# The last u pair of a Conformer and retention decoder kernel, computed as the first of 21 units of seven half-size products

## What is computed

```python
proj = rms_norm(x) @ w_in                       # 1024 x 6144
a_val, a_gate, q, k, v, g, gate_a, gate_b = split(proj)
u = a_val * sigmoid(a_gate)                     # 512 channels
conv = depthwise_conv31(concat(history, u)) + b_dw
a_out = silu(layer_norm(conv)) @ w_conv_out
o = retention(rotary(q), rotary(k), v)          # chunks of 128, 4 heads
b_out = (silu(g) * rms(o)) @ w_ret_out
h = x + rms_norm((sigmoid(gate_a) * a_out + sigmoid(gate_b) * b_out) @ w_o)
y = h + rms_norm(relu(rms_norm(h) @ w_up)**2 @ w_down)
```

## Time and profile before

| | |
|---|---|
| median of three runs | 1497.71 us (1497.56 to 1498.16) |
| profiled execution: span, first to last instruction | 1495.6 us |
| its mean granted TensorE clock | 0.997 |
| busy TensorE / VectorE / POOL / ACT | 99% / 67% / 56% / 42% |
| third pair begins, first unit begins, second unit begins | 60.95, 106.41, 127.19 us |

### The profile page before, as it was taken

The page is one execution under the profiler, slowest core; times in us unless marked ns, Lnnn a source line. Parts: engine busy times, 40 slices in busy tenths (PEclk is TensorE's granted clock), DMA queues, the critical chain, the costliest instruction groups (busy, mean ns, idle before and its releaser), DMA issues.

```text
span 1495.6 us, 28307 instructions
## 1 busy us (share of the span) xinstructions
PE 1475.2 (99%) x11336; PEld 1455.2 (97%) x11336; DVE 1001.0 (67%) x1251; ACT 635.4 (42%) x929; POOL 842.0 (56%) x571
## 2 busy tenths in 40 slices
PE   8999999999999999999999999999999999999996
PEld 5999999999999999999999999999999999999995
DVE  7999888856545724576715876766657765574847
ACT  5533444344544541131213855556556332332333
POOL 3377776777545653257565445555555655554555
PEclk9999999999999999999999999999999999999998
DMA  6013333322356258621421144566759575454634
GB/s 217 22 42 94 114 114 113 113 80 65 112 176 205 75 200 296 219 80 50 149 78 50 29 149 171 199 237 219 253 193 326 203 285 189 142 208 156 227 107 170
DMA packets 110091, 229.13 MB, mean 153 GB/s; under 512 B 8960, under 2 KB 20992, under 8 KB 108304
## 3 DMA queue, kind: packets, MB, share of 16 engines
q1 hardware_dynamic: 95296, 204.30, 39.7%
q10 hardware_dynamic: 14672, 23.09, 4.6%
HBM read 154.41 MB, written 72.95 MB: 152 GB/s over the span
## 4 chain that ended last, share of the span: by engine, by line
PE 96%; POOL 1%; DMA 1%; ACT 1%; issue 1%; DVE 0%; POOLq 0%; SPq 0%; DVEq 0%; ACTq 0%
PE ps L1476 40%; PE ps L1237 26%; PE ps L1026 16%; PE ps L1402 3%; PE ps L1389 3%; PE ps L1074 2%; PE ps L1164 1%; PE ps L1169 1%; PE ps L1180 1%; PE ps L1166 1%; DMA cva_h<-conv_scratch 1%; PE ps L1147 0%; PE ps L1152 0%; PE ps L1194 0%; POOL w_l L931 0%
## 5 line engine op out<-in xcount | busy, mean ns | idle before, releaser
L1476 PE MATMUL ps<-tx_h,w_h 128*128 128x258 f32 x960 | 271.5, 283 | 0.0
L1476 PE MATMUL ps<-tx_l,w_h 128*128 128x258 f32 x960 | 271.3, 283 | 0.0
L1476 PE MATMUL ps<-tx_h,w_l 128*128 128x258 f32 x960 | 271.1, 282 | 0.0
L996 POOL TENSOR_TENSOR w_l<-raw,w_h 128x512 fp32r<-128x512 f32 x120 | 185.6, 1551 | 147.6 <-ACT w_h L2033 147.1
L1476 PE MATMUL ps<-fx_l,w_h 128*128 128x258 f32 x720 | 203.7, 283 | 0.0
L1476 PE MATMUL ps<-fx_h,w_h 128*128 128x258 f32 x720 | 203.6, 283 | 0.0
L1476 PE MATMUL ps<-fx_h,w_l 128*128 128x258 f32 x720 | 203.4, 282 | 0.0
L1476 PEld LDWEIGHTS ps<-tx_h,w_h 128*128 128x128 f32 x960 | 181.4, 189 | 0.1
L1476 PEld LDWEIGHTS ps<-tx_l,w_h 128*128 128x128 f32 x960 | 181.4, 189 | 0.1
L1476 PEld LDWEIGHTS ps<-tx_h,w_l 128*128 128x128 f32 x960 | 181.2, 189 | 0.0
L2328 DVE SCALAR_TENSOR_TENSOR ps<-u_ext,wdw,ps 128x512 f32<-128x512 f32 x232 | 155.2, 749 | 0.0
(11 more groups left out here) (386 smaller groups left out, 4305.4 us busy)
## 6 DMA issues: line engine op xcount, KB each, us to landing
raw<-wseq_dram SPq DMA_DIRECT2D x260, 256.0 KB, 3.1
quad_scratch<-quad_h SPq DMA_DIRECT2D x16, 774.0 KB, 3.5
tx_h<-quad_scratch SPq DMA_DIRECT2D x12, 1032.0 KB, 10.4
tx_l<-hidden_scratch SPq DMA_DIRECT2D x12, 1032.0 KB, 12.8
gate_scratch<-gst SPq DMA_DIRECT2D x10, 1032.0 KB, 5.0
hidden_scratch<-hq_g SPq DMA_DIRECT2D x8, 1032.0 KB, 7.0
hidden_scratch<-stg_b SPq DMA_DIRECT2D x6, 1032.0 KB, 6.9
hq_g<-hidden_scratch SPq DMA_DIRECT2D x6, 1032.0 KB, 13.1
```

The costliest lines, as they stand in the source:

```text
L996: pool.tensor_tensor(lo, src, hi.bitcast(F32), ALU.subtract).then_inc(q_lo, 1)
L1476: out = pe.matmul(ps[:, 2 * n + s, 0:HC], RINGS[q % RING][wa][:, kk * P:(kk + 1) * P], OPS[x][xb][:, QK * kh + kk, at_:at_ + HC], start=(i ...
```

## The change

Pair 3 is computed as unit 0 of 21 (`X_U = 0`); all other units move one number up. Slots 12 to 15 of the weight stream are now loaded, split and summed as a unit's. The eight half sums of x stand two behind each of the low parts of slots 8, 9 and 10, the seventh behind the first weight sum, the eighth between the third and the fourth low part of unit 0. On ACT the high parts of operands 2 and 3 stand behind slot 10's and slot 11's, 5 ahead of the third weight, 4 within unit 0. VectorE makes 2, 3, 5 and 4 in this order between fewer taps: 17 instead of 29 taps stand before the units, nine in unit 0, ten in unit 1 and eleven in each of units 2 to 9. Gate products are now in units 2 to 5. The product of gate and value of tile 3, and its sample part, stand at the head of unit 1 on VectorE (`u_unit_out`), behind two sigmoids of ACT. The two conv outputs leave one unit later. The first group of the convolution's output product starts with two of its three chunks and takes the third when its bank is free.

```diff
-XU = 20
+XU = 21
-G_AOUT, S_AOUT = 9, 16
+G_AOUT, S_AOUT = 7, 12
+X_U = 0
+U_SLOTS = 12
+OPERAND_AT = {2: 1, 3: 2, 5: 3, 4: 4}
...
@@ POOL
-            for n in range(RAW, 16):
-                if n == 15:
-                    unit_sum(0, 0)
+            for n in range(RAW, U_SLOTS):
                 low_part(n % RAW, n)
                 if n == 2 * RAW:
                     pool.wait_ge(xs_sc, KT)
-                    x_sum(0)
-                if 2 * RAW <= n < 15:
-                    x_sum(n - 2 * RAW + 1)
+                if 2 * RAW <= n < U_SLOTS - 1:
+                    x_sum(2 * (n - 2 * RAW))
+                    x_sum(2 * (n - 2 * RAW) + 1)
+            unit_sum(0, 0)
+            x_sum(6)
...
                 unit_low(v, 2)
+                if v == 0:
+                    x_sum(7)
                 unit_low(v, 3)
@@ TensorE
-            with pe.Fori(0, CT - 2) as i:
-                group8(G_U + 4, S_U + 8, XN, i, i * 4)
-                group8(G_U + 5, S_U + 10, XN, i, i * 4)
+            group8(G_U + 4, S_U + 8, XN)
+            group8(G_U + 5, S_U + 10, XN)
...
-                    taken(pe, G_U + 6 + k)
+                    taken(pe, G_U + 4 + k)
...
                 if v == 0 and 2 <= i <= 5:
-                    pe.wait_ge(xs_lo, i - 1)
+                    pe.wait_ge(xs_lo, OPERAND_AT[i])
...
-                    x_evicted(pe, XU - 1, ("e2", "e7")[c])
-                    x_evicted(pe, XU - 1, "e5")
+                    x_evicted(pe, XU - 1, ("e5", "e2")[c])
@@ ACT
             weight_hi(10)
             x_operand_hi(2)
+            u_gate(2)
             weight_hi(11)
-            u_gate(2)
-            weight_hi(12)
             x_operand_hi(3)
-            weight_hi(13)
-            weight_hi(14)
-            x_operand_hi(4)
-            u_gate(3)
-            weight_hi(15)
...
                 unit_high(v, 4)
+                if v == X_U:
+                    x_operand_hi(4)
...
+                if v == X_U:
+                    x_evicted(act, v, "e2")
+                    act.activation(x_row(v, 0), x_row(v, 0), ACT.Sigmoid).then_inc(u_sg, 1)
...
             unit_high(0, 0)
             unit_high(0, 1)
+            x_operand_hi(5)
             unit_high(0, 2)
-            x_operand_hi(5)
@@ VectorE
             taps(10)
             u_out(1)
             u_sample(1)
-            taps(11)
+            taps(3)
+            x_operand_lo(2)
+            taps(2)
+            x_operand_lo(3)
+            taps(2)
             u_out(2)
             u_sample(2)
-            x_operand_lo(2)
-            taps(8)
-            x_operand_lo(3)
-            u_out(3)
-            x_operand_lo(4)
             x_operand_lo(5)
-            u_sample(3)
...
+                dve.wait_ge(u_sg, 1)
+                for name in ("e5", "e6", "e7"):
+                    x_evicted(dve, X_U, name)
+                for t in range(2):
+                    at_ = HIST + t * HT
+                    dve.tensor_tensor(u_ext[:, CT - 1, at_:at_ + HT], x_row(X_U, 2 + t), x_row(X_U, t), ALU.mult
+                                      ).then_inc(u_x, 1)
+                dve.wait_ge(u_x, 2)
+                u_sample(CT - 1)
...
                 if v < X_KQ[0][0]:
-                    if j == 1:
-                        taps(4 if v < 5 else 5)
-                    if j == 5 and v < 5:
-                        taps(1)
-                    if j == 6:
-                        taps(5 if v < 4 else 6)
+                    if v == X_U:
+                        if j == 1:
+                            x_operand_lo(4)
+                            taps(4)
+                        if j == 6:
+                            taps(5)
+                    else:
+                        if j == 1:
+                            taps(4 if v < 6 else 5)
+                        if j == 5 and v < 6:
+                            taps(1)
+                        if j == 6:
+                            taps(5 if v < 2 else 6)
+                if (v, j) == (X_U + 1, 0):
+                    u_unit_out()
```

More of the change, by code:

```diff
@@ L404, in build @@
         y_st = sem("y_st")
+        u_sg = sem("u_sg")
+        u_x = sem("u_x")
         def done(slot):
@@ L459, in x_loads @@
         def x_loads(v):
-            return 16 * (16 // RAW + v)
+            return 16 * (U_SLOTS // RAW + v)
         XBANKS = [(2, 1, 0)]
@@ L483, in x_rows @@
         def x_rows(v, r, n):
-            if v in X_GATES:
+            if v in X_GATES or v == X_U:
                 k = 4 * (v % 2) + r
-                if v in (13, 14):
-                    k = 4 * (v - 13) + r
+                if v == X_GB[3]:
+                    k = 4 + r
+                if v in X_GB[1:3]:
+                    k = 4 * X_GB[1:3].index(v) + r
                     return gst_c[:, k:k + n, :]
@@ L611, in _ @@
             sp.dma_start(x_in[:, :, 2 * CH:T], xT[:, :, 2 * CH:T]).then_inc(x2_ld, 16)
-            sp.dma_start(hist[:], cacheT).then_inc(hist_ld, 16)
-            for n in range(2 * RAW, 16):
+            sp.dma_start(hist[:], cacheT).then_inc(wdw_ld, 16)
+            for n in range(2 * RAW, U_SLOTS):
                 sp.wait_ge(w_split, n - RAW + 1)
@@ L1294, in _ @@
                 if c == 0:
-                    for n, sub in enumerate((2, 3, 0, 1)):
+                    for n, sub in ((0, 2), (1, 3)):
+                        pe.wait_ge(piece_ld[sub], CV_LD + 16)
+                        for a in range(2):
+                            for b in (1, 2):
+                                pe.matmul(pch(g, b), W[a][:, slot % HL, sub * P:(sub + 1) * P],
+                                          cva_h[:, sub, b * CH:(b + 1) * CH], start=(n == 0 and a == 0), stop=False)
+                    x_evicted(pe, XU - 1, "e7")
+                    for n, sub in ((0, 2), (1, 3)):
+                        for a in range(2):
+                            pe.matmul(pch(g, 0), W[a][:, slot % HL, sub * P:(sub + 1) * P],
+                                      cva_h[:, sub, 0:CH], start=(n == 0 and a == 0), stop=False)
+                    for n, sub in ((2, 0), (3, 1)):
                         pe.wait_ge(piece_ld[sub], CV_LD + 16)
@@ L1299, in _ @@
                                 pe.matmul(pch(g, b), W[a][:, slot % HL, sub * P:(sub + 1) * P],
-                                          cva_h[:, sub, b * CH:(b + 1) * CH], start=(n == 0 and a == 0), stop=False)
+                                          cva_h[:, sub, b * CH:(b + 1) * CH], start=False, stop=False)
                         if n == 2:
-                            x_evicted(pe, XU - 1, "e7")
                             pe.wait_ge(on_n, 6)
@@ L1825, in unit_out @@
                 if v == 0:
-                    taken(act, G_U + 7)
+                    taken(act, G_U + 5)
                 if v == 1:
                     act.wait_ge(xs_lo, 4)
+                if v == 2:
+                    act.wait_ge(u_x, 2)
                 if v in X_KQ[1]:
@@ L2244, in square_half @@
                 if c:
-                    dve.wait_ge(x_sq, 2 * c + half - 1)
+                    dve.wait_ge(x_sq, 2 * c + half + 3)
                 else:
-                    dve.wait_ge(x0_sq, 2 * half + 2)
+                    dve.wait_ge(x_sq, 2 * half + 2)
                 return dve.tensor_tensor(q[:, a:a + 2], q[:, a:a + 2], q[:, a + 2:a + 4], ALU.add)
```

70 lines of the change are left out of this document (34 added, 36 removed).

## The result

The changed kernel takes 1502.46 us (1501.73 to 1502.65), the kernel before in the same runs 1497.73: a ratio of 1.0029, 95% interval 1.0020 to 1.0039. It is slower by 4.7 us, where the forecast was 5.1. The profiled execution spans 1500.6 us, against 1495.6.

The account below looks back on a forecast made before the run. TensorE bounds the kernel, and the change makes it wait for POOL's full queue: 8.1 us of waits less 0.6 and 2.5 gives +5.1, so 1497.7 + 5.1 = 1502.8 us, range 1499.0 to 1505.0.

Parts of the forecast that it names:

- The gain: On TensorE, a 22.73 us pair becomes a 20.21 us unit: 2.52 us saved, at most 3.1 with 0.57 us of waits gone.
- POOL's queue: From 58.87 us to the fourth product's low part: 31.5 us of work, ready at 90.4, wanted at 92.3, slack 1.9 us.
- Who gets the port: VectorE's four all-SBUF low parts each go between two back-to-back POOL instructions, holding POOL 4 x 2.25 = 9.0 us.
- The waits: TensorE waits for POOL's last-slot low part and the first unit's first, fourth and fifth products: 8.1 us in all.
- The bounds: Waits between 5.9 and 8.1 us, so change between +2.8 and +5.1, upper end taken; some other costs taken as nothing.
- the sample at the head of the second unit: Last u tile's sample part may delay the row addition freeing the seventh product's bank: 0.7 us by layout, nothing taken.
- the twelve taps: Taps moved behind, making eleven a unit in units 2 to 5 on VectorE: costed at nothing, though with thin cover.
- (a): Rival: VectorE's low parts fit into POOL's pauses, no wait grows: 1494.6 us, or 1495.2 with some waits; chance 0.05.
- (b): Rival: half of it collides, two of four low parts, 3.6 us of waits less 3.1: 1498.2 us; chance 0.12.
- (d): Rival: VectorE, not POOL, is late, the second product waiting for the u product, adding 1 to 2: 1504; chance 0.08.
- (c): Rival: the clock falls to 1.2 GHz in the 3.0 us stop, +1.0 to +3.9: 1503.8 to 1506.7 us; chance 0.07.

Follow-up runs that it names:

- before_sums_on_dve: The kernel before, with the eight sums of x on VectorE, three low parts in one go and seven taps later: 1496.62 us, ratio 0.9993.
- sums_on_dve: The changed kernel with the eight sums of x on VectorE instead of POOL, low parts regrouped, seven taps later: 1494.71 us, ratio 0.9982 against the kernel before.
- sums_early: The changed kernel with POOL's sums of x begun after four of the eight gains, which come reordered: 1496.72 us, ratio 0.9995 against the kernel before.
- taps_later: The changed kernel with seven VectorE taps moved from between the low parts into units 6 to 9: 1501.14 us.
- lows_together: sums_early with VectorE's second to fourth operands' low parts in one go, seven taps later, the last slot's high part behind two operand parts on ScalarE: 1499.74 us.
- w11_lows_ahead: lows_together with the last slot's high part back ahead on ScalarE and the first unit's first two low parts ahead of its weight sums on POOL: 1499.12 us.
- before_pool_plus: The kernel before plus two unused 512-column POOL instructions behind the sixth sum of x, counted in ScalarE's raised wait: 1500.06 us, ratio 1.0014.
- before_pool_late: The kernel before plus two extra 512-column POOL instructions behind the eighth sum of x, ScalarE's waits unchanged: 1497.42 us, ratio 0.9998.
- pool_plus: The changed kernel plus two more 512-column POOL instructions behind the sixth sum of x, ScalarE's wait raised to count them: 1503.55 us.

## Why the prediction was right

- **The gain.** 22.73 - 20.21 = 2.52 us, capped at 3.1 with the old waits. Shown: the pair of runs with no waits on POOL, before_sums_on_dve and sums_on_dve, lies 1.9 us apart with 0.6 us of waits in the second.
- **POOL's queue.** Ten short instructions and eight sums, 31.5 us, with 1.9 us of slack. POOL was busy 42.53 of 43.50 us; the durations laid out (2.38, 1.25) stood. sums_early, which starts the queue sooner, and sums_on_dve, which takes the sums out of it, both end the loss.
- **Who gets the port.** Two of the four turns went as laid out. At the fourth product the order was the other: operand 5's low part came ahead of the eighth sum (92.51 against 92.53 us), not behind it; the sum of the two is the same. At the fifth product too: I had the fourth operand's low part first and then the weight sum; its high part waited for the eighth sum on ScalarE (97.08 us), so the weight sum went first. Again the three add up alike.
- **The waits.** Laid out 1.7, 1.5, 3.0 and 1.9 us; from start to start, less the matmuls between, 1.18, 1.15, 2.70 and 1.75. Sum 8.1 against 6.8, or 7.3 by the whole stretch, so that the change comes to +4.2 us there and not +5.1. The step that was mis-sized is the first: the last slot's low part was to end 18.9 us behind the third pair's start and ended 18.2 behind it. The sample part of the second tile had ended 0.4 us sooner than I let it, and all behind moved with it. By the fifth product the layout was 0.95 us late (41.50 us behind the pair's start, 42.45 laid out). That the median still came within 0.4 us of the forecast is in part luck: 0.5 us of it lies outside the stretch.
- **The bounds.** Nothing for the sample at the head of the second unit: right, VectorE's row addition at 121.91 us made nobody wait. Nothing for the twelve taps: right, there is no wait over 0.3 us behind 140 us.
- **The rivals.** (a) and (b): W is 7.3 us and all four low parts collide. (d): taps_later. (c), the clock: in the profiled execution it was granted at 1.00 in each 2-us window from 92 to 104, the 2.54-us stop among them. The rule of TensorE: Matmul & The Clock Gate in the Trainium skill, in its section "Why this matters for your kernels", as the prediction gave it (idle gaps cost the clock), isn't seen in it, but it is seen in lows_together and w11_lows_ahead. Nor is it out for the executions without a profile: the mean granted clock is 0.996 or 0.997 in every execution of the kernel before for which it is recorded, but 0.995, 0.995 and 0.994 in three of the seven of the changed kernel. These three took 1502.39 to 1502.65 us, the profiled one 1502.50, so it cost little. That rival was nearer than its 0.07 makes it look. Its price was too high: a product at half clock was put at 5.77 us, but w11_lows_ahead starts its matmuls of 258 columns 0.215 us apart there (0.12 at the full clock), which makes 5.2 us for 24.
- **What stays open beside the sum.** The prediction read POOL's 9.9 us of waiting for ScalarE as pauses that the new queue no longer has. That the new queue has next to none is shown (42.53 of 43.50 us). How much of the old pauses was room is not: before_pool_plus put 2.3 us there and lost 2.5, but through a wait of ScalarE that its own edit raised, and before_pool_late, without that wait and later, lost nothing.

## What to carry to other kernels

Before work is moved earlier, lay out the queue of the engine that prepares it, with each collision at the shared port as a full instruction of the other engine. Ask of each of its instructions who waits for it: where the waiting engine is the one that gives this engine its next work, a delay comes back and isn't swallowed by the idle time behind it. If the queue is full, start it sooner (sums_early, 5.7 us here) or move work to the engine that is faster at it and give that engine's least urgent work away (sums_on_dve, 7.8 us). The one shift of order within the queue that was tried alone, w11_lows_ahead, only moved the wait. Run the new layout under the old kernel too, or its gain is put down to the wrong edit. And when instructions are added to price an engine's work, see that no other engine's wait counts them in.

## What the runs showed of the hardware that was not expected

- A VectorE low part with one operand in PSUM takes the same 2.30 us as with both in SBUF, but POOL's instruction beside it takes 1.30 instead of 3.3 us. Only who reads what decides, not how long.
- The same subtraction of 128x1032 fp32 takes 1.23 us on VectorE and 2.4 on POOL.
- The length of TensorE's stop alone doesn't tell whether the clock falls. Stops of 2.54 us (changed kernel) and 3.02 (pool_plus) left it at 1.00; stops of 2.20 (w11_lows_ahead) and 3.27 (lows_together) were followed by some 3 us at half clock, 1.5 and 1.65 us dearer. What decides stays open. The times of both kernels split accordingly wide: 1497.7 to 1500.3 and 1497.7 to 1504.4, where the others stay within 2 us. The mean granted clock of each execution goes with it: 0.997 in the two of lows_together at 1497.7 to 1497.8 us and 0.994 to 0.996 in the nine from 1499.5 on; 0.996 or 0.997 in the five of w11_lows_ahead up to 1498.2 us, and 0.995 in five of the six above (0.996 in one). That the split is the clock is thus likely, and not shown in a trace, since one execution of each was profiled; one such stretch of 1.65 us wouldn't explain the 1504.4.
